# Splitting the out-projection of the SSD's even steps into two halves, one on either side of the projection of z

## The chip, the core and the metric

The kernel runs on one core of a Trainium2 chip. Its five engines work at the same time and meet through semaphores: PE (TensorE, the matrix multiplier), DVE (VectorE), ACT (ScalarE), POOL (GpSimd) and SP, which issues the DMAs. The metric is the time of one execution on the device in microseconds (us), lower being better.

## What is computed

An encoder of two layers over two request groups of 256 and 512 tokens, 768 in all, with D = 1024. The first layer mixes with a bidirectional Mamba-2 (SSD) branch, the second with neighbourhood attention. The change is in the SSD branch, which is, cut to what matters:

```python
z, xbc, dt_f, dt_b, q_mem = split(h @ w_in)
xs, bm, cm = split(silu(conv5(xbc)))                  # centred depthwise convolution, 5 taps
y = ssd_forward(xs, bm, cm, dt_f) + ssd_backward(...) + d_skip * xs
y = rmsnorm(y * silu(z), norm_g)                      # 2048 channels
x = x + rmsnorm(concat([y, m]) @ w_out)               # m: memory attention
```

Within a chunk of 128 tokens a direction is `(C B^T * decay) @ x`, and between chunks a state is carried.

## The kernel before, in words

The 2048 channels of the branch are 32 heads, taken as 16 pairs of 128 channels. The loop `for n in range(PAIRS)` of `ssd_phase` handles one pair in each step n = 0 to 15. Every matrix is multiplied in three float32r products (high*high, low*high, high*low), so a tile named `Mh`, `Wh` or `Hh` has a partner `Ml`, `Wl` or `Hl`.

Weights come in units of 512 KB. SP loads a unit into one of two slots of `Wraw` (L161 to L168), POOL splits it into `Wh` and `Wl` with two instructions (L188, L191), PE uses it and raises `unit_done`, and that lets POOL split the unit after the next. A unit is either "dense" (`pe_dense`, L200: 24 matmuls over 256 columns and 24 over 512) or half of an out-projection (`pe_out_tiles`, L251: six token tiles of six 512-column matmuls each, 36 in all). Each out tile goes to one of two PSUM banks in turn, so the third tile waits until DVE has added the first to `acc` (`out_added`, L261; the adds are L298, or copies at L296 for the first pair of channels).

An even step n from 2 on also carries the out-projection of the pairs n-2 and n-1. Before the change the order on PE in such a step is:

1. the dense unit of the next pair's x (L214), with six transposes of this pair's x (L1684) between its two parts;
2. the states (16 matmuls, L1713) and the column sums of squares (12 matmuls with one output column each, L1690);
3. the dense unit of z (L214), which ACT evicts with a SiLU;
4. `pe_out` (L280): a wait for `mix_ready`, then two halves of 36 matmuls (L264), columns 0 to 511 and 512 to 1023 of the output;
5. y (L1743 and L1747), which waits for `dec_ready`, `cs_ready` and `carried` of DVE.

On DVE the same step is: scaling x (L1536), in steps 4, 8 and 12 the masks of the group (L1552), the two operations on `seg` (L1558, L1561), `low_part(n-1)` (L1524), which makes the low part of the mixed values of pair n-1 and raises `mix_ready`, the four multiplies of `cs` (L1572), the two decay multiplies (L1577, L1578), the states carried (L1585), the adds of both halves (L298) with the four convolution taps of the next pair's x (L1168) among them, and last y (L1627), y times z (L1630) and `low_part(n)`. "The decays" below are L1577 and L1578. In the order of SP the step has the units x, z, first half, second half and then the load of the next `ab` (L1056).

Steps 2, 4, 6, 8, 10 and 12 have this form; step 14 and step 15 handle their halves in another way, which the change leaves alone.

Of the kernel before, what the change touches and what calls it, by code (L numbers as in the profile page):

```python
# [80 lines left out]
def encoder_kernel(nc, x_prompt, x_sample, mem_prompt, mem_sample, pre_g, post_g, mem_g, w_mem_kv, w_out,  # L81
# [3 lines left out]
    with ctx:  # L85
# [1201 lines left out]
        def ssd_phase(phase, pre, nxt, mixes):  # L1287
# [42 lines left out]
            def out_in(n):  # L1330
                return n % 2 == 0 and n >= 2

            def dense_index(n):
                return 4 + sum((m < LAST) + group_unit(m) + 1 for m in range(n))

# [21 lines left out]
                return evicted(dense_index(n) + (n < LAST) + group_unit(n))  # L1357

            def out_unit(n):
                return unit0 + unit_index(n) + (n < LAST) + group_unit(n) + 1  # L1360

            def sync(sp):
                load_x, load_b, load_c = pre.loads(sp)

                def load_ab(n):
                    sp.wait_ge(ab_exp, n)
                    sp.wait_ge(seg_ready, n)
                    pre.load_ab(sp, n)

                for n in range(PAIRS):  # L1370
                    if 0 < n < LAST:
                        load_x(n + 1)
                    if group_unit(n):
                        load_b(n // 4 + 1)
                        load_c(n // 4 + 1)
                    if n:
                        load_f(sp, w_in, slice(n * P, (n + 1) * P))
                    if out_in(n) and n < LAST - 1:
                        load_out(sp, 0, slice((n - 2) * P, n * P))
                    elif n >= LAST - 1:  # L1380
                        load_unit(sp, w_out[0, 12 * P:14 * P, (n % 2) * 512:(n % 2 + 1) * 512]
                                  .rearrange("(k p) c -> p k c", p=P), 2)
                    if n < LAST:
                        load_ab(n + 1)
                    if n == 1:
                        sp.wait_ge(padded, 32)
                        for rr in range(15):
                            src = bass.AP(rp_dram.tensor, (14 - rr) * 80 + 31, [[1200, HEADS], [-1, 16], [1, 32]])
                            sp.dma_start(gs_dram[:, :, rr, :], src).then_inc(expanded, 16)
                    if n == 2:  # L1390
                        for rr in range(7):
                            src = bass.AP(rp_dram.tensor, (10 - rr) * 80 + 31, [[1200, HEADS], [-1, 32], [1, 48]])
                            sp.dma_start(gp_dram[:, :, rr, :], src).then_inc(expanded, 16)
                sp.wait_ge(silu_done, x_silu(LAST))
                for i in range(3):
                    nxt.load_mem(sp, i)
                sp.wait_ge(gated, LAST)
                sp.wait_ge(x_scaled, PAIRS)
                nxt.load_mem(sp, 3)
                sp.wait_ge(ab_exp, PAIRS)  # L1400
                sp.wait_ge(seg_ready, PAIRS)
                nxt.load_mem_gain(sp)
                load_out(sp, 0, slice(14 * P, 16 * P))
# [6 lines left out]
            def scalar(act):  # L1410
# [13 lines left out]
                for n in range(PAIRS):  # L1424
                    g, a = n // 4, n % 2
                    act.wait_ge(ab_landed, 16 * (n + 1))
                    if n:
                        act.wait_ge(y_done, n)
                    else:
                        act.wait_ge(padded, 16)  # L1430
                        act.wait_ge(pre.mixed, 12)
                    for d, dst in enumerate((F_DST, B_DST)):
                        for s0, s1 in ((0, 1), (1, 4)):
                            i = act.activation(cs[:, d, :, s0:s1, :].rearrange("p h s l -> p h (s l)"),
                                               ab[:, d, :, dst[s0] * P:(dst[s1 - 1] + 1) * P], ACT.Exp)
                    i.then_inc(ab_exp, 1)

                    def decay():
                        act.wait_ge(seg_ready, n + 1)
                        for ch in range(NT):  # L1440
                            for h in range(2):
                                at = 32 + 2 * n + h
                                i = act.activation(seg[:, ch, h, :], seg[:, ch, h, :], ACT.Exp,  # L1443
                                                   bias=acs_tok[:, ch, at:at + 1])
                        i.then_inc(seg_exp, 1)

                    j = conv_index(n)
                    if n < LAST:
                        take_raw(j, n + 1)
                    decay()  # L1450
                    if n == LAST:
                        act.wait_ge(sq_summed, n)
                        take_spans(act, z, ACT.Silu)
                        U["act"].next()

                    act.wait_ge(states_done, n + 1)
                    act.activation(prev[:, 0, 0:2, :], A[2][:, 0:256].rearrange("p (s f) -> p s f", f=P), ACT.Copy)
                    act.activation(prev[:, 1, 0, :], A[3][:, 0:P], ACT.Copy)
                    act.activation(prev[:, 1, 3, :], A[3][:, 3 * P:4 * P], ACT.Copy).then_inc(prev_set, 1)
                    if next_group(n):  # L1460
                        take_bt(g + 1)

                    if group_unit(n):
                        take_raw(j + 1, g + 17)
                        silu(j, n + 1, xs[1 - a])
                        take_raw(j + 2, g + 21)
                        act.wait_ge(bc_done, g + 1)
                        silu(j + 1, g + 17, bT)
                    if n < LAST:
                        if n:  # L1470
                            act.wait_ge(sq_summed, n)
                        take_spans(act, z, ACT.Silu)
                    if group_unit(n):
                        silu(j + 2, g + 21, cT[1 - g % 2])
                    elif n < LAST:
                        silu(j, n + 1, xs[1 - a])

                    def square():
                        act.activation(z, y, ACT.Square).then_inc(sq_done, 1)

                    if n == LAST:
                        act.wait_ge(ab_exp, PAIRS)
                        nxt.mem_sums(act)
                    act.wait_ge(gated, n + 1)
                    if n < LAST:
                        square()
                    if out_in(n):
                        U["act"].next()
                        if n < LAST - 1:
                            act.wait_ge(unit_done, out_unit(n) + 2 + 2)  # L1490
                            U["act"].next()
                    act.activation(mix(n)[0], y, ACT.Copy, scale=cw[:, n + 144:n + 145]).then_inc(hi_ready, 1)
                    if n == LAST:
                        square()
# [9 lines left out]
            def vector(dve):  # L1504
# [25 lines left out]
                for n in range(PAIRS):  # L1530
# [42 lines left out]
                                                  .broadcast_to([P, 2, t1 - t0]), ALU.mult)  # L1573
                    i.then_inc(cs_ready, 1)

                    dve.wait_ge(seg_exp, n + 1)
                    c.add(dve.tensor_tensor(dec, seg, both_heads(cb_u), ALU.mult))  # L1577
                    dve.tensor_tensor(seg, seg, both_heads(cb_l), ALU.mult).then_inc(dec_ready, 1)  # L1578
# [15 lines left out]
                                else:  # L1594
                                    c.add(i)

                    j, dense = conv_index(n), dense_index(n)
                    if n == LAST:
                        nxt.mem_roots(dve, c)
                        nxt.mem_norm.dve_normed(dve, 0)  # L1600
# [2 lines left out]
                    elif n == LAST - 1:  # L1603
                        U["dve"].k = out_unit(n)
                        dve.wait_ge(dense_free, evicted(dense))
                        for i, tiles in enumerate(((0, 1), (2, 3), (4, 5), ())):
                            tap(j, n + 1, i)
                            dve_out_tiles(dve, 0, tiles)
                    elif out_in(n):
                        U["dve"].k = out_unit(n)  # L1610
                        dve.wait_ge(dense_free, evicted(dense))
                        if n == 2:
                            dve.wait_ge(stored, 16)
                        for half in range(2):
                            dve_out(dve, (half,), first=(n == 2), then=lambda k: tap(j, n + 1, 2 * half + k) if n < LAST else None)
                    elif n < LAST:
                        conv5(j, n + 1, dense)
                    if group_unit(n):
# [37 lines left out]
            def tensor(pe):  # L1656
# [39 lines left out]
                for n in range(PAIRS):  # L1696
# [21 lines left out]
                        squares(n - 1)  # L1718
                    if next_group(n):
                        turn_b(g + 1)  # L1720
                    if n < LAST:
                        for _ in range(group_unit(n) + 1):
                            pe_dense(pe)
# [5 lines left out]
                        pe_mixed(pe)  # L1729
                        pe_out_tiles(pe, range(NT))  # L1730
                    elif out_in(n):
                        pe_out(pe)

                    if n:
                        pe.wait_ge(gated, n)
# [522 lines left out]
```

## Time and profile before

| | us |
|---|---|
| median of 3 runs (lowest, highest) | 2225.23 (2225.05, 2226.71) |
| the profiled execution | 2223.82 |
| its span, first to last instruction | 2221.9 |

The span is what the profile shows; 1.9 us lie around it. A row of a timeline is: start in us from the span's start, duration in us, engine, line, operation, output and inputs, count, and in brackets the idle time before it with what ended it. A matmul's duration is longer than its distance to the next one, since matmuls are pipelined: the work is read from starts.

### The profile page before, as it was taken

To read this page: it belongs to the slowest core of one execution; us is meant where nothing else is said; L and a number is where in the kernel's file an instruction comes from. 1 tells how busy PE (TensorE), PEld (TensorE's weight loads), DVE (VectorE), ACT (ScalarE), POOL (GpSimd) and SP (SyncE) were. 2 spreads that over 40 slices of the span, in tenths; PEclk is the share of its full clock that TensorE was granted. 3 is DMA by queue.
4 is the path that set the end of the run, shared out by engine and by line. 5 is a ranking of instruction groups with operands and counts; after the bars stand their busy time and mean duration, and the time that the engine had idled before them with its cause. 6 is when DMAs were issued, how large, how long until landed. Compare 5 with 4: busy or idle time off the path is not lost.

```text
span 2221.9 us, 32088 instructions
## 1 busy us (share of the span) xinstructions
PE 2145.5 (97%) x13298; PEld 1845.3 (83%) x13298; DVE 1078.0 (49%) x1677; ACT 731.5 (33%) x1665; POOL 929.7 (42%) x623
## 2 busy tenths in 40 slices
PE   6999999999999999997999999999999999999997
PEld 5888887888888888886788887888888888888885
DVE  3103333688887888886721323234233334334236
ACT  4123122344353444343332212242324233232343
POOL 4543333332433433333753332754444445454444
PEclk9999999999999999998999999999999999999999
DMA  5221112334222232233431111322221222212211
GB/s 183 92 69 51 53 54 80 123 95 120 86 92 79 78 104 76 95 104 116 161 133 57 48 57 47 106 96 61 63 60 56 66 61 61 72 50 65 66 48 67
DMA packets 216396, 180.57 MB, mean 81 GB/s; under 512 B 23387, under 2 KB 188539, under 8 KB 216251
## 3 DMA queue, kind: packets, MB, share of 16 engines
q1 hardware_dynamic: 216251, 178.52, 25.6%
q8 instruction: 105, 1.72, 0.3%
q14 instruction: 40, 0.33, 0.1%
HBM read 168.71 MB, written 12.21 MB: 81 GB/s over the span
## 4 chain that ended last, share of the span: by engine, by line
PE 78%; DVE 15%; ACT 3%; issue 2%; DMA 1%; POOL 0%; SPq 0%; DVEq 0%; POOLq 0%; ACTq 0%
PE bank L214 44%; PE bank L264 16%; PE bank L910 4%; DVE R L1168 3%; PE bank L2143 2%; PE bank L2158 2%; PE bank L936 2%; DVE R L1536 2%; PE bank L2133 2%; PE bank L1743 1%; ACT R L1443 1%; PE bank L974 1%; DVE R L1558 1%; PE bank L1747 1%; DVE R L1578 1%
## 5 line engine op out<-in xcount | busy, mean ns | idle before, releaser
L214 PE MATMUL bank<-Hh,Wh 128*128 128x256 f32 (+1 forms) x2192 | 753.3, 344 | 7.6 <-ACT R L1107 5.1
L188 POOL TENSOR_SCALAR Wh<-Wraw 128x1024 fp32r<-128x1024 f32 x217 | 250.2, 1153 | 1215.6 <-issue 812.7
L214 PE MATMUL bank<-Hl,Wh 128*128 128x256 f32 (+1 forms) x2192 | 739.2, 337 | 0.0
L214 PE MATMUL bank<-Hh,Wl 128*128 128x256 f32 (+1 forms) x2192 | 738.0, 337 | 0.0
L191 POOL TENSOR_TENSOR Wl<-Wraw,Wh 128x1024 fp32r<-128x1024 f32 x217 | 551.0, 2539 | 18.1
L214 PEld LDWEIGHTS bank<-Hh,Wh 128*128 128x128 f32 x2192 | 417.0, 190 | 58.5 <-issue 13.6
L214 PEld LDWEIGHTS bank<-Hh,Wl 128*128 128x128 f32 x2192 | 416.5, 190 | 44.3
L214 PEld LDWEIGHTS bank<-Hl,Wh 128*128 128x128 f32 x2192 | 417.0, 190 | 41.2 <-issue 1.9
L298 DVE TENSOR_TENSOR acc<-bank,acc 128x512 f32<-128x512 f32 x240 | 164.8, 691 | 173.8 <-PE bank L264 173.1
L264 PE MATMUL bank<-Wh,Mh 128*128 128x512 f32 x528 | 210.8, 399 | 22.5 <-DVE acc L298 22.5
L264 PE MATMUL bank<-Wh,Ml 128*128 128x512 f32 x528 | 207.6, 393 | 0.0
L264 PE MATMUL bank<-Wl,Mh 128*128 128x512 f32 x528 | 207.1, 392 | 0.0
L246 ACT ACTIVATE R<-bank 128x512 f32<-128x512 f32 x78 | 46.6, 597 | 316.4 <-PE bank L214 316.4
L1168 DVE SCALAR_TENSOR_TENSOR R<-R 128x770 f32<-128x770 f32 x96 | 140.3, 1467 | 13.5 <-ACT R L1107 11.8
L264 PEld LDWEIGHTS bank<-Wh,Mh 128*128 128x128 f32 x528 | 100.0, 189 | 50.9 <-DVE acc L298 28.9
L2032 DVE TENSOR_TENSOR R<-bank,R 128x256 f32<-128x256 f32 (+1 forms) x32 | 24.9, 859 | 225.2 <-PE bank L2158 225.2
L1932 ACT ACTIVATE R<-R 128x256 f32<-128x256 f32 (+2 forms) x192 | 86.4, 452 | 137.4 <-DVE R L2058 137.4
L1902 POOL TENSOR_TENSOR R<-R 128x160 f32<-128x160 f32 (+2 forms) x160 | 108.8, 716 | 42.5 <-DVE R L2058 42.4
L2023 DVE TENSOR_SCALAR R<-R 128x256 f32<-128x256 f32 (+2 forms) x192 | 122.3, 703 | 1.1
L850 DVE TENSOR_REDUCE R<-bank 128x2 f32<-128x512 f32 x24 | 16.6, 692 | 214.6 <-PE bank L936 214.6
L264 PEld LDWEIGHTS bank<-Wl,Mh 128*128 128x128 f32 x528 | 100.3, 190 | 21.5
L264 PEld LDWEIGHTS bank<-Wh,Ml 128*128 128x128 f32 x528 | 100.3, 190 | 19.8
(232 smaller groups left out, 2726.6 us busy)
## 6 DMA issues: line engine op xcount, KB each, us to landing
Wraw<-in_na_w_in_dram SPq DMA_DIRECT2D x80, 512.0 KB, 3.6
Wraw<-in_ssd_w_in_dram SPq DMA_DIRECT2D x57, 512.0 KB, 3.8
Wraw<-in_w_out_dram SPq DMA_DIRECT2D x48, 512.0 KB, 3.5
R<-acs_dram SPq DMA_DIRECT2D x16, 1536.0 KB, 6.2
Wraw<-in_w_mem_kv_dram SPq DMA_DIRECT2D x32, 512.0 KB, 3.9
R<-gs_dram SPq DMA_DIRECT2D x32, 128.0 KB, 3.4
macc_dram<-acc SPq DMA_DIRECT2D x1, 3072.0 KB, 9.5
R<-macc_dram SPq DMA_DIRECT2D x6, 512.0 KB, 4.4
```

The lines of the kernel that those rows point to most:

```text
L188: pool.tensor_scalar(Wh[:, s, :], Wraw[:, s, :], 1.0, 1.0, ALU.mult, ALU.mult).then_inc(pool_c, 1)
L191: pool.tensor_tensor(Wl[:, s, :], Wraw[:, s, :], Wh[:, s, :].bitcast(F32), ALU.subtract)\
L214: mm = pe.matmul(DB[h.k % 2][:, 0:t1 - t0], w[:, k, :], x[:, k, t0:t1], start=(k == 0 and i == 0), stop=(k == KC - 1 and i == 2))
L246: lambda b: act.activation(dst[:, NP_:T], b[:, 0:NS], func, scale=scale)])
L264: mm = pe.matmul(A[4 + o.k % 2][:, :], x[k][:, i * P:(i + 1) * P], w[:, k, :], start=(k == 0 and j == 0), stop=(k == 1 and j == 2))
L298: dve.tensor_tensor(dst, A[4 + o.k % 2][:, :], dst, ALU.add).then_inc(out_added, 1)
L910: mm = pe.matmul(V_BANK[t][:, :], x[:, 2 * j + k, tok], y[:, k, :], start=(j == 0 and k == 0 and p == 0), stop=(j == 3 and k == 1 and p == 2))
L936: mm = pe.matmul(A[t // 2][:, (t % 2) * 256:(t % 2 + 1) * 256], qm[:, k, t * P:(t + 1) * P], kT[:, h * 2 + k, group[t] * 256:(group[t] + 1 ...
L1168: i = dve.scalar_tensor_tensor(o, x[:, k:k + w], self.cw[:, m + 24 * k:m + 24 * k + 1], o, ALU.mult, ALU.add)
L1902: i = pool.tensor_tensor(o, m, src, ALU.add)
L1932: i = act.activation(s, s, ACT.Exp, bias=nmax[:, o, h:h + 1], accum_out=sums[:, o, h:h + 1])
L2023: i = dve.tensor_scalar(s, s, rinv[:, o, h:h + 1], None, ALU.mult)
```

## The change

In the steps 2 to 12 that are even (`out_around_z`), the first half of the out-projection, with the wait for `mix_ready`, is put ahead of the dense unit of z on PE, and the second half stays behind it. SP loads the units in the order x, first half, z, second half. On DVE the first half's six adds, with two of the four taps, stand behind the multiplies of `cs` and ahead of the decays; the second half's adds with the other two taps stay where both were. ACT counts its units to match. No operation is added or left out.

```diff
+            def out_around_z(n):
+                return out_in(n) and n < LAST - 1
...
             def out_unit(n):
-                return unit0 + unit_index(n) + (n < LAST) + group_unit(n) + 1
+                return unit0 + unit_index(n) + (n < LAST) + group_unit(n) + (not out_around_z(n))
...
+                    if out_around_z(n):
+                        load_unit(sp, w_out[0, (n - 2) * P:n * P, 0:512].rearrange("(k p) c -> p k c", p=P), 2)
                     if n:
                         load_f(sp, w_in, slice(n * P, (n + 1) * P))
-                    if out_in(n) and n < LAST - 1:
-                        load_out(sp, 0, slice((n - 2) * P, n * P))
+                    if out_around_z(n):
+                        load_unit(sp, w_out[0, (n - 2) * P:n * P, 512:1024].rearrange("(k p) c -> p k c", p=P), 2)
...
                     i.then_inc(cs_ready, 1)
+
+                    j, dense = conv_index(n), dense_index(n)
+
+                    def adds(half):
+                        U["dve"].k = out_unit(n) + 2 * half
+                        dve_out(dve, (half,), first=(n == 2), then=lambda k: tap(j, n + 1, 2 * half + k))
+
+                    if out_around_z(n):
+                        dve.wait_ge(dense_free, evicted(dense))
+                        if n == 2:
+                            dve.wait_ge(stored, 16)
+                        adds(0)
 
                     dve.wait_ge(seg_exp, n + 1)
...
                     elif out_in(n):
-                        U["dve"].k = out_unit(n)
-                        dve.wait_ge(dense_free, evicted(dense))
-                        if n == 2:
-                            dve.wait_ge(stored, 16)
-                        for half in range(2):
-                            dve_out(dve, (half,), first=(n == 2), then=lambda k: tap(j, n + 1, 2 * half + k) if n < LAST else None)
+                        adds(1)
...
+                    if out_around_z(n):
+                        pe_mixed(pe)
+                        pe_out_tiles(pe, range(NT))
                     if n < LAST:
                         for _ in range(group_unit(n) + 1):
                             pe_dense(pe)
...
                     elif out_in(n):
-                        pe_out(pe)
+                        pe_out_tiles(pe, range(NT))
```

On PE, at the point in step 6 where the sums of squares end, the kernel before goes on with z (`Wh` and `Hh`, the projected input):

```order
L1713 MATMUL bank<-R 128x128 x8
L1690 MATMUL bank<-ones,R 128x1 x6
L214 MATMUL bank<-Hh,Wh 128x256
L214 MATMUL bank<-Hl,Wh 128x256
L214 MATMUL bank<-Hh,Wl 128x256
```

The changed kernel goes on with the first half (`Wh` and `Mh`, the mixed values):

```order
L1725 MATMUL bank<-R 128x128 x8
L1702 MATMUL bank<-ones,R 128x1 x6
L264 MATMUL bank<-Wh,Mh 128x512
L264 MATMUL bank<-Wh,Ml 128x512
L264 MATMUL bank<-Wl,Mh 128x512
```

Thirty-six matmuls of the out-projection now stand between the sums of squares and z; 36 are left behind z. The line numbers past the first edit have moved (L1713 is L1725, L1690 is L1702).

On DVE, step 6 from `low_part(5)` on, in the kernel before:

```order
L1524 SCALAR_TENSOR_TENSOR Ml<-R,Mh 128x768
L1572 TENSOR_TENSOR R<-R 128x2x128
L1572 TENSOR_TENSOR R<-R 128x2x384
L1572 TENSOR_TENSOR R<-R 128x2x128
L1572 TENSOR_TENSOR R<-R 128x2x384
L1577 TENSOR_TENSOR R<-R 128x1536
L1578 TENSOR_TENSOR R<-R 128x1536
L1585 SCALAR_TENSOR_TENSOR R<-R,bank 128x64 x8
L298 TENSOR_TENSOR acc<-bank,acc 128x512 x2
L1168 SCALAR_TENSOR_TENSOR R<-R 128x770
L298 TENSOR_TENSOR acc<-bank,acc 128x512 x3
```

And in the changed kernel, from the last multiply of `cs` on:

```order
L1578 TENSOR_TENSOR R<-R 128x2x384
L298 TENSOR_TENSOR acc<-bank,acc 128x512 x2
L1168 SCALAR_TENSOR_TENSOR R<-R 128x770
L298 TENSOR_TENSOR acc<-bank,acc 128x512 x3
L1168 SCALAR_TENSOR_TENSOR R<-R 128x770
L298 TENSOR_TENSOR acc<-bank,acc 128x512
L1595 TENSOR_TENSOR R<-R 128x1536
L1596 TENSOR_TENSOR R<-R 128x1536
L1603 SCALAR_TENSOR_TENSOR R<-R,bank 128x64 x8
L298 TENSOR_TENSOR acc<-bank,acc 128x512 x2
L1168 SCALAR_TENSOR_TENSOR R<-R 128x770
```

Six adds and two taps have moved ahead of the decays and of the carried states; `low_part` and the multiplies of `cs` are still ahead of every add. (L1578 of the changed kernel is L1572 of the one before.)

## Rows read from the trace of the kernel before

**Rows 1.** The page: busy time of each engine, and the chain's shares by engine.
```profile
PE 2145.5 (97%) x13298; PEld 1845.3 (83%) x13298; DVE 1078.0 (49%) x1677; ACT 731.5 (33%) x1665; POOL 929.7 (42%) x623
...
PE 78%; DVE 15%; ACT 3%; issue 2%; DMA 1%; POOL 0%; SPq 0%; DVEq 0%; POOLq 0%; ACTq 0%
```
**Rows 2.** Windows, first z matmul to first y matmul: steps 2, 4, 6, 8, 12.
```profile
core 0: us, PE busy (x) PEld busy (x) DVE busy (x) ACT busy (x) POOL busy (x), PEclk, DMA share, GB/s
504.49:529.68 25.19, 25.19 (x122) 20.59 (x121) 21.09 (x30) 5.06 (x14) 9.43 (x5) 1.00 0.62 156
573.48:603.17 29.69, 26.89 (x122) 21.72 (x122) 23.98 (x31) 6.37 (x18) 10.81 (x5) 0.94 0.33 107
663.39:688.58 25.19, 25.19 (x122) 20.59 (x121) 21.09 (x30) 5.06 (x14) 9.43 (x5) 1.00 0.30 101
732.38:759.16 26.78, 25.38 (x122) 20.58 (x121) 23.35 (x31) 6.48 (x18) 12.14 (x5) 1.00 0.37 118
...
889.75:916.23 26.48, 25.38 (x123) 20.58 (x122) 23.04 (x31) 6.48 (x18) 11.58 (x5) 1.00 0.31 100
```
**Rows 3.** Timeline of PE in step 4.
```profile
572.22 1.40 PE L1690 MATMUL bank<-ones,R 128*128 128x1 f32 x12
...
581.90 0.39 PE L264 MATMUL bank<-Wh,Mh 128*128 128x512 f32 x1
...
587.59 0.74 PE L264 MATMUL bank<-Wh,Mh 128*128 128x512 f32 x1 [2.80 <-DVE acc L298]
```
**Rows 4.** Timeline of DVE in step 4.
```profile
577.23 1.00 DVE L1524 SCALAR_TENSOR_TENSOR Ml<-R,Mh 128x768 fp32r<-128x768 f32 x1
578.16 2.49 DVE L1572 TENSOR_TENSOR R<-R 128x256 f32<-128x256 f32 x4
...
586.85 1.28 DVE L298 TENSOR_TENSOR acc<-bank,acc 128x512 f32<-128x512 f32 x2
```
**Rows 5.** Timeline of PE in step 6: the first out matmul.
```profile
671.82 0.39 PE L264 MATMUL bank<-Wh,Mh 128*128 128x512 f32 x1
```
**Rows 6.** Timeline of DVE in step 6.
```profile
661.86 1.79 DVE L1524 SCALAR_TENSOR_TENSOR Ml<-R,Mh 128x768 fp32r<-128x768 f32 x1
663.57 4.70 DVE L1572 TENSOR_TENSOR R<-R 128x256 f32<-128x256 f32 x4
668.19 1.75 DVE L1577 TENSOR_TENSOR R<-R 128x1536 f32<-128x1536 f32 x1
...
688.87 0.69 DVE L298 TENSOR_TENSOR acc<-bank,acc 128x512 f32<-128x512 f32 x1
```
**Rows 7.** Timeline of POOL in step 6.
```profile
660.70 2.14 POOL L188 TENSOR_SCALAR Wh<-Wraw 128x1024 fp32r<-128x1024 f32 x1 [10.23 <-issue]
662.93 2.99 POOL L191 TENSOR_TENSOR Wl<-Wraw,Wh 128x1024 fp32r<-128x1024 f32 x1
```
**Rows 8.** Timeline of DVE in steps 8 and 12.
```profile
736.96 2.48 DVE L1572 TENSOR_TENSOR R<-R 128x256 f32<-128x256 f32 x4
739.36 1.75 DVE L1577 TENSOR_TENSOR R<-R 128x1536 f32<-128x1536 f32 x1
...
894.02 2.48 DVE L1572 TENSOR_TENSOR R<-R 128x256 f32<-128x256 f32 x4
896.43 1.75 DVE L1577 TENSOR_TENSOR R<-R 128x1536 f32<-128x1536 f32 x1
```
**Rows 9.** Timeline of PE: two more waits, in steps 1 and 8.
```profile
477.81 0.36 PE L214 MATMUL bank<-Hh,Wh 128*128 128x256 f32 x1 [2.25 <-ACT R L1107]
...
745.09 0.50 PE L264 MATMUL bank<-Wh,Mh 128*128 128x512 f32 x1 [1.40 <-DVE acc L298]
```
**Rows 10.** Windows behind the waits of rows 3 and 9.
```profile
478.50:481.80 3.30, 3.30 (x18) 3.30 (x17) 3.23 (x4) 1.36 (x3) 2.50 (x2) 0.50 0.44 111
587.70:591.00 3.30, 3.30 (x8) 2.62 (x9) 1.80 (x3) 0.00 (x0) 0.00 (x0) 0.50 0.57 159
745.00:770.00 25.00, 24.91 (x182) 21.23 (x183) 16.00 (x21) 5.00 (x7) 8.01 (x5) 1.00 0.23 64
```

More of the change, by code:

```diff
@@ L1468, in scalar @@
                         silu(j + 1, g + 17, bT)
+                    if out_around_z(n):
+                        U["act"].next()
                     if n < LAST:
@@ L1489, in scalar @@
                         if n < LAST - 1:
-                            act.wait_ge(unit_done, out_unit(n) + 2 + 2)
-                            U["act"].next()
+                            act.wait_ge(unit_done, out_unit(n) + 3 + 2)
                     act.activation(mix(n)[0], y, ACT.Copy, scale=cw[:, n + 144:n + 145]).then_inc(hi_ready, 1)
@@ L1595, in vector @@
                                     c.add(i)
-                    j, dense = conv_index(n), dense_index(n)
                     if n == LAST:
@@ L1720, in tensor @@
                         turn_b(g + 1)
+                    if out_around_z(n):
+                        pe_mixed(pe)
+                        pe_out_tiles(pe, range(NT))
                     if n < LAST:
```

## The prediction

> **What bounds the kernel now.** I read the page first: PE is busy for 97% of the span and holds 78% of the chain that ended last [rows 1]. So the kernel ends when PE ends, and an edit that only moves instructions can do no more than open or close waits of PE. Next I took the windows of the changed steps, from the first matmul of z to the first of y, which hold the same work in each: z and 72 matmuls of the out-projection. They take 25.19 us in steps 2 and 6 (step 10 is alike), but 29.69, 26.78 and 26.48 in steps 4, 8 and 12 [rows 2]. Taking 25.19 as the time without waits, before loses 4.50 + 1.59 + 1.29 = 7.4 us there. That is all that the change can win in these windows.
>
> The timelines say what the loss is. In step 4 the first out tile begins at 581.90, and the third after a wait of 2.80 us for DVE's first add [rows 3]; that add is late because `low_part`, the multiplies of `cs`, the decays and the carried states stand ahead of it, and the adds begin at 586.85 [rows 4]. Steps 8 and 12 show the same with 1.40 (the row of step 8 is in [rows 9]). In steps 2, 6 and 10 DVE is in time.
>
> **What the change does, part by part.** *Work.* Nothing is added: the same matmuls, adds, taps and loads. Their durations count for nothing but through waits. *Loads and splits.* A unit keeps its place in the row of units and only the content of the second and third changes, so POOL's splits start at the same events (the end of the unit two before). I cost this at 0: the second unit of a step is split before the step's first ends, whatever it holds. *ACT* takes z some 8.4 us later (from the start of z at 663.39 [rows 2] to the first out matmul at 671.82 [rows 5] is 8.43 for a dense unit, and (25.19 - 8.43)/2 = 8.38 for a half), and DVE needs z only behind y, which comes another half later: 0. *The decays* must be done before y. Behind the last add of the first half they have z and the second half on PE, 16.8 us, as cover. With the carried states they lie in step 4 between 580.65 and 586.85 [rows 4], 6.2 us with a split of POOL beside them: 0 for y. They also stand ahead of the second half's adds; that is weighed below.
>
> *The first half's start.* It needs `mix_ready`, which `low_part` of the pair before raises; the edit moves the wait ahead of z and moves nothing on DVE ahead of `low_part`. This is where the change costs. In step 4 the squares begin at 572.22 and z at 573.48; `low_part` ends at 577.23 + 1.00 = 578.23 [rows 3, 4]. z now covers none of that time: PE stands for 4.7 us, with z, the second half and y queued behind it in order. In steps 8 and 12 `low_part` ends where the multiplies of `cs` begin, at 737.0 and 894.1 [rows 8], against 732.38 and 889.75 for z before [rows 2]: waits of 4.7 and 4.4 us. In step 6 it ends at 663.65 against 663.39 [rows 2, 6]: 0.3 us; steps 2 and 10 are alike to 0.05 us (the same pattern, read from the same view).
>
> *The third tile.* It needs the first add, which now stands right behind the multiplies of `cs`. An add takes 0.69 us [rows 6], and PE followed the add in step 4 by 0.05 us (586.85 + 0.69 = 587.54, next matmul 587.59) [rows 3, 4]. A tile is 8.38/6 = 1.40 us, so without a wait the third starts 2.79 us behind the first. The delay of a whole first half is then the start of its third tile less (start of z before + 2.79):
> - Step 6: the adds can start where L1577 did, 668.19 [rows 6]; third tile at 668.19 + 0.69 + 0.05 = 668.93, less 666.18 = 2.75. Steps 2 and 10 the same: 8.25 for three.
> - Step 4: the multiplies are done at 580.65 and the next operation could start at 580.57 (rows overlap by 0.08) [rows 4]; third tile at 581.31 less 576.27 = 5.04.
> - Step 8: 739.36 + 0.74 = 740.10, less 735.17 = 4.93 [rows 8]. Step 12: 896.43 + 0.74 = 897.17, less 892.54 = 4.63 [rows 8].
>
> The sum is 22.85 us. Later tiles do not wait again: an add and a tap make 1.7 us for two tiles of 1.4. The old waits disappear, since z stands between the halves and the decays lie beside it: -7.4. Net +15.4 us before the clock is counted.
>
> *The clock.* Behind the waits of 2.25 us in step 1 and of 2.80 in step 4 PE's granted clock is 0.50, the lower of its two levels (1.2 GHz), for at least 3.3 us; behind the 1.40 in step 8 it stays at 1.00 [rows 9, 10]. In step 4 that cost 4.50 less the wait itself (587.59 - 581.90 - 2.79 = 2.90), so 1.60 us [rows 2, 3]. The new waits: one of 4.4 to 4.7 us in each of steps 4, 8 and 12, and one of about 2.3 us (0.2 more ahead of it) in each of 2, 6 and 10 (the second tile's end near 666.6, the third's start at 668.93). The cost of the clock behind each lies between 0 and, if it stays low twice as long, 3.2. All six are at or above the 2.25 that was followed by a slow stretch, so I take 1.60 each, 9.6 in all. Part of a slow stretch can fall within the longer waits, where it costs nothing; for that I take off 1.5 in all, my choice, about one stretch of the six.
>
> **The sum.** 2223.82 (the profiled execution) + 15.4 + 9.6 = 2248.8; the median of the runs shown is 1.4 above that execution, 2250.2; less the 1.5 just named, 2248.7. I forecast 2249 us, +1.1%.
>
> **A rule weighed.** POOL's split began as x's unit ended in step 6, and both engines ran long: L191 took 2.99 us, and the four multiplies took 4.70 us against 2.49 in step 4 [rows 4, 6, 7]. L191 ran until 665.92, so the multiplies that began at 663.57 had 2.2 us to lose, and 2.2 is what they lost. The Trainium skill, "SBUF — State Buffer", section "SBUF: two separate sides", says that VectorE instructions with two SBUF inputs and GpSimd share one pair of ports under an exclusive lock, held for a whole instruction, while the loser waits. By that rule, with which the trace agrees, the change can do harm in a second place, since the decays now start just as the first half's end releases a split; what that would make is rival 4.
>
> **Rivals.**
> 1. *The waits come, the clock does not fall behind the short ones.* For it: 2.3 us is right at the shortest that was followed by a slow stretch, 2.25 [rows 9, 10]. Then 3 x 1.60 go: 2223.8 + 15.4 + 4.8 + 1.4 = 2245.4. With none anywhere: 2240.6.
> 2. *POOL no longer meets the multiplies in steps 2, 6, 10.* Then these take 2.49 instead of 4.70, and the third tile is late by 0.5 instead of 2.75: -6.7, and what is left of the short waits is too short for the clock, -4.8; from 2250.2 that makes 2238.7. Against it: the split and the multiplies both hang on the end of x's unit, which does not move.
> 3. *Faster: the first half's start is not late.* Place: the wait for `mix_ready` in steps 4, 8, 12. If DVE reached `low_part` there by the end of the squares, and the multiplies of `cs` did not hold the first add, PE would lose nothing where it now loses 7.4: 2217.8. It decides from the point where the six first halves lose less than 7.4 us together, 1.2 each; by the rows they lose 2.75 to 5.04. Against it: DVE does not start a changed step earlier than before, since the last add follows PE's last tile in both orders (688.87 + 0.69 against 688.58 for y in step 6 [rows 2, 6]).
> 4. *Worse: the decays hold the second half, and the clock stays low for longer.* The decays and carried states begin 1.0 us behind the first half's end (the last add ends at 689.56 where the halves end at 688.58 [rows 2, 6]) and take 6.2 us as in step 4: done at 7.2. The second half's third tile is due 8.43 + 2.79 = 11.2 us behind that end and its add must begin 0.74 sooner, at 10.5, so 3.3 us are spare. A whole further L188 and L191 (2.14 + 2.99 [rows 7]) would use them up and make 1.8 us late in each step, 11 in six; one of the two would not. Beside it each long wait could bring twice the slow stretch: +4.8. So 2253.5 with the clock alone, up to 2264 with both. Against the first: step 4's 6.2 us have a split in them already.
> 5. *The change is not what it says.* The rows of the order show the 36 matmuls and the six adds moved, so I give this nothing of its own.
>
> **Chances and range.** Forecast with its clock (2246 to 2252) 0.55; rival 1 0.22; rival 2 0.07; rival 4 0.09; rival 3 0.03; 0.04 for something that levels out to no change. A measurement of this kernel can tell about 0.2%, 4.5 us, from no change. Slower than that are the forecast and rivals 1, 2 and 4: 0.93. The range from 2238 to 2256 takes in rivals 1 and 2 and the nearer part of 4, and leaves out rival 3, no change, and the far part of 4.
>
> **What would show it.** In the profile after: PE idle 4 to 5 us ahead of the first L264 in steps 4, 8 and 12, ended by DVE's `low_part`; about 2.3 us ahead of the third tile in steps 2, 6 and 10, ended by the add; no wait of PE in any second half; about 23 us of such delay against 7.4; and granted clock 0.50 behind these waits, five stretches more than before. I am wrong if PE's first L264 follows the squares at once in step 4, if the decays or y come to hold PE, or if the time is under 2235.

## The result, and the profile after

| | us |
|---|---|
| before, median of 4 runs (lowest, highest) | 2225.97 (2225.05, 2227.89) |
| after, median of 4 runs (lowest, highest) | 2248.95 (2248.44, 2251.52) |
| ratio, with its 95% interval | 1.0104 [1.0087, 1.0122] |
| span of the profiled execution, before and after | 2221.9 and 2247.0 |

The change costs 1.0%. The page after, where [rows 1] were, has the same instructions:

```profile
PE 2153.9 (96%) x13298; PEld 1851.2 (82%) x13298; DVE 1092.4 (49%) x1677; ACT 731.7 (33%) x1665; POOL 932.5 (42%) x623
```

PE gives up a point of its share. The windows of the changed steps say where. They begin where z would begin without a wait, which is 1.26 us behind the start of the sums of squares (as in [rows 3], 572.22, and [rows 2], 573.48), and end at the first matmul of y, so they hold the same work as [rows 2]. Columns as there:

```profile
506.12:533.98 27.86, 25.50 (x123) 20.72 (x122) 23.12 (x30) 5.05 (x14) 10.78 (x5) 1.00 0.58 139
577.77:609.38 31.61, 27.00 (x123) 22.07 (x122) 25.54 (x31) 6.48 (x18) 10.42 (x5) 0.89 0.32 101
669.62:699.04 29.42, 27.06 (x122) 21.88 (x121) 23.11 (x30) 5.05 (x14) 10.78 (x5) 0.94 0.26 87
744.38:776.03 31.65, 27.46 (x123) 22.39 (x122) 25.11 (x31) 6.47 (x18) 11.73 (x5) 0.89 0.31 100
836.27:865.74 29.47, 27.11 (x122) 21.85 (x121) 23.10 (x30) 5.05 (x14) 10.77 (x5) 0.94 0.25 86
910.69:942.81 32.12, 27.93 (x123) 22.76 (x122) 25.11 (x31) 6.47 (x18) 11.73 (x5) 0.89 0.25 82
```

Less 25.19 each, the six steps lose 2.67, 6.42, 4.23, 6.46, 4.28 and 6.93 us, 31.0 in all, against 7.4 before. That is 23.6 of the 25.1 us between the spans. The rest lies outside the windows: PE was 1.6 us later already at the sums of squares of step 1 (459.00 against 457.38), which the change does not reach. That is the spread of single executions: in e1 below, the same up to there, the squares begin at 457.51.

PE's waits in steps 2 to 12 carry these names (totals of PE's waits between 425 and 980 us; the second and third count the adds and, in step 2, the copies):

```profile
PE bank L264 <- DVE Ml L1530: 13.5, 6, 4.6
...
PE bank L264 <- DVE acc L298: 4.4, 2, 2.2
...
PE bank L264 <- DVE acc L296: 2.2, 1, 2.2
```

L1530 is `low_part` (L1524 before). PE's timeline of steps 4 and 6 has them one by one; they answer to [rows 3] and [rows 5]:

```profile
576.51 1.40 PE L1702 MATMUL bank<-ones,R 128*128 128x1 f32 x12
582.52 0.79 PE L264 MATMUL bank<-Wh,Mh 128*128 128x512 f32 x1 [4.61 <-DVE Ml L1530]
```
```profile
668.36 1.40 PE L1702 MATMUL bank<-ones,R 128*128 128x1 f32 x12
669.93 0.50 PE L264 MATMUL bank<-Wh,Mh 128*128 128x512 f32 x1 [0.17 <-DVE Ml L1530]
...
675.14 0.79 PE L264 MATMUL bank<-Wh,Mh 128*128 128x512 f32 x1 [2.19 <-DVE acc L298]
```

The second half has no wait in any step. DVE in step 6, as in [rows 6], shows who ends the wait and what follows; POOL's rows beside it answer to [rows 7]:

```profile
668.08 1.79 DVE L1530 SCALAR_TENSOR_TENSOR Ml<-R,Mh 128x768 fp32r<-128x768 f32 x1
669.80 4.69 DVE L1578 TENSOR_TENSOR R<-R 128x256 f32<-128x256 f32 x4
674.41 1.28 DVE L298 TENSOR_TENSOR acc<-bank,acc 128x512 f32<-128x512 f32 x2
...
683.39 1.90 DVE L1595 TENSOR_TENSOR R<-R 128x1536 f32<-128x1536 f32 x1
685.21 3.95 DVE L1596 TENSOR_TENSOR R<-R 128x1536 f32<-128x1536 f32 x1
689.09 1.73 DVE L1603 SCALAR_TENSOR_TENSOR R<-R,bank 128x64 f32<-128x64 f32 x8
```
```profile
669.15 2.98 POOL L191 TENSOR_TENSOR Wl<-Wraw,Wh 128x1024 fp32r<-128x1024 f32 x1
682.63 1.05 POOL L188 TENSOR_SCALAR Wh<-Wraw 128x1024 fp32r<-128x1024 f32 x1 [10.50 <-issue]
683.77 3.77 POOL L191 TENSOR_TENSOR Wl<-Wraw,Wh 128x1024 fp32r<-128x1024 f32 x1
...
692.10 2.40 POOL L191 TENSOR_TENSOR Wl<-Wraw,Wh 128x1024 fp32r<-128x1024 f32 x1
```

The first add waits for four multiplies that L191 stretches to 4.69 us, just as in [rows 6]. The granted clock (third column from the right, as in [rows 10]) in the five stretches where it is low:

```profile
579.40:586.20 6.80, 3.67 (x9) 2.90 (x10) 6.12 (x7) 4.21 (x15) 0.53 (x1) 0.51 0.48 172
675.00:678.30 3.30, 3.16 (x8) 2.48 (x9) 1.74 (x4) 0.00 (x0) 0.00 (x0) 0.51 0.24 72
746.70:753.40 6.70, 4.69 (x11) 3.73 (x12) 5.06 (x6) 3.17 (x12) 1.14 (x1) 0.51 0.89 313
842.30:845.60 3.30, 3.30 (x9) 2.58 (x9) 1.65 (x3) 0.00 (x0) 0.00 (x0) 0.51 0.05 16
913.90:920.70 6.80, 5.68 (x13) 4.46 (x14) 4.32 (x7) 2.28 (x9) 0.25 (x1) 0.51 0.76 270
```

Step 2 has none, although its wait is as long as that of step 6 (2.19 us both).

### The profile page after: what moved, and what is told of

Its sections match the earlier page's. It is cut to its first block, busy times and chain, and to the rows that moved or that the text cites. A ratio compares the mean times of both kernels' runs of the same rounds, so it can differ in the third digit from the quotient of the medians.

```text
span 2247.0 us, 32088 instructions
## 1 busy us (share of the span) xinstructions
PE 2153.9 (96%) x13298; PEld 1851.2 (82%) x13298; DVE 1092.4 (49%) x1677; ACT 731.7 (33%) x1665; POOL 932.5 (42%) x623
## 4 chain that ended last, share of the span: by engine, by line
PE 77%; DVE 16%; ACT 3%; issue 3%; DMA 1%; POOL 0%; SPq 0%; DVEq 0%; POOLq 0%; ACTq 0%
PE bank L214 43%; PE bank L264 16%; PE bank L910 4%; DVE R L1168 3%; DVE R L1542 2%; PE bank L2158 2%; PE bank L2173 2%; PE bank L936 2%; PE bank L2148 2%; PE bank L1758 1%; DVE R L1564 1%; PE bank L974 1%; DVE R L1578 1%; ACT R L1448 1%; DVE Ml L1530 1%
## 5 line engine op out<-in xcount | busy, mean ns | idle before, releaser
L188 POOL TENSOR_SCALAR Wh<-Wraw 128x1024 fp32r<-128x1024 f32 x217 | 244.4, 1126 | 1237.7 <-issue 849.5
L191 POOL TENSOR_TENSOR Wl<-Wraw,Wh 128x1024 fp32r<-128x1024 f32 x217 | 559.7, 2579 | 18.1
```

The costliest lines, as they stand in the source:

```text
L188: pool.tensor_scalar(Wh[:, s, :], Wraw[:, s, :], 1.0, 1.0, ALU.mult, ALU.mult).then_inc(pool_c, 1)
L191: pool.tensor_tensor(Wl[:, s, :], Wraw[:, s, :], Wh[:, s, :].bitcast(F32), ALU.subtract)\
```

## The experiments

Every kernel below ran beside the kernel before on the same chip; its ratio is to that. The delay per step is worked out from each trace as above: from the start of the sums of squares to the first matmul of y, less 26.45 us (662.13 to 688.58, step 6 of the kernel before). The 26.45 us are not quite free of small gaps, so values can lie a little below zero: in step 6 of e8 the 72 out matmuls take 16.54 us (8.29 + 8.25) where they took 16.76 before, and z 8.35 where it took 8.43.

| kernel | steps 2, 4, 6, 8, 10, 12: delay, us | sum | ratio to before [95%] |
|---|---|---|---|
| before | 0.0, 4.5, 0.0, 1.6, 0.1, 1.3 | 7.4 | 1 |
| changed | 2.7, 6.4, 4.2, 6.5, 4.3, 6.9 | 31.0 | 1.0104 [1.0087, 1.0122] |
| e1 adds early | 0.8, 6.5, 0.7, 7.7, 0.8, 7.4 | 23.9 | 1.0083 [1.0067, 1.0099] |
| e2 low part early | 4.0, 6.6, 4.2, 5.7, 4.1, 6.8 | 31.3 | 1.0103 [1.0085, 1.0122] |
| e3 both early | 0.8, 2.2, 0.4, 2.2, 0.4, 2.2 | 8.2 | 1.0006 [0.9996, 1.0016] |
| e4 PE filled | 2.7, 4.6, 2.8, 4.6, 2.7, 4.6 | 22.1 | 1.0087 [1.0072, 1.0102] |
| e5 PE's move alone | 9.3, 12.0, 10.2, 12.6, 10.3, 11.9 | 66.3 | 1.0256 [1.0240, 1.0273] |
| e6 DVE's move alone | 7.8, 8.6, 7.7, 8.6, 7.7, 7.8 | 48.2 | 1.0194 [1.0172, 1.0215] |
| e7 woven | 2.2, 2.2, 2.1, 2.2, 2.2, 2.2 | 13.1 | 1.0038 [1.0024, 1.0052] |
| e8 carried states split | -0.3, 0.3, -0.3, 0.3, -0.3, 0.3 | 0.0 | 0.9966 [0.9953, 0.9978] |
| e9 split only | -0.3, 1.5, -0.3, 1.5, -0.3, 1.5 | 3.5 | 0.9980 [0.9970, 0.9990] |

**e1: the first adds ahead of the multiplies of cs.**

```diff
+                    if out_around_z(n):
+                        ...
+                        adds(0)
                     dve.wait_ge(ab_exp, n + 1)
...
-                    if out_around_z(n):
-                        ...
-                        adds(0)
                     dve.wait_ge(seg_exp, n + 1)
```

> The changed kernel, with the first half's adds also ahead of the multiplies of cs (before: behind them). Theory A (in steps 2, 6, 10 PE waits at the third tile because the first add stands behind these multiplies; in 4, 8, 12 the wait for mix_ready dominates): the 2.2 us waits go, the waits of 4.2 to 4.6 us ahead of the first half stay. 3 x 2.5 + 3 x 0.2 us and two slow stretches of 1.6 less: about 2238, up to 2245 if the decays, now later still, hold the second half. Theory B (all of the loss hangs on mix_ready): 2249, no change.

Median 2241.52. Steps 2, 6 and 10 fall from 2.7, 4.2, 4.3 to 0.7 or 0.8; steps 4, 8, 12 keep theirs or lose a little more (7.7 against 6.5 in step 8), with the wait for `low_part` (4.20 us in step 4). Theory A holds, B does not. A wait of 0.38 us has come into every second half: the multiplies of cs now lie with the decays, and the second half's first add is late.

**e2: low_part early.**

```diff
+                    if n and n % 2 == 0:
+                        low_part(n - 1)
                     if n % 4 == 0:
                         dve.wait_ge(bc_done, g + 1)
...
-                    if n and n % 2 == 0:
-                        low_part(n - 1)
```

> The changed kernel, with low_part(n-1) moved from behind the two operations on seg to right behind the scaling of x, so mix_ready comes 4 to 9 us earlier. Theory A (third tile is bound by the first add behind cs, whose place in time hardly moves): the idle time of 4.2 to 4.6 us ahead of the first half in steps 4, 8, 12 goes and comes back as one of about the same length at the third tile; 2247 to 2250. Theory B (mix_ready is the cost): three waits of 4.3 us and three slow stretches go, 13 to 18 us: 2231 to 2236.

Median 2247.12, delay 31.3 against 31.0 us. The wait for `mix_ready` has gone and its time stands one event later. PE and DVE in step 4:

```profile
584.76 0.80 PE L264 MATMUL bank<-Wh,Mh 128*128 128x512 f32 x1 [3.92 <-DVE acc L298]
```
```profile
577.86 3.83 DVE L1570 TENSOR_TENSOR R<-R 128x1536 f32<-128x1536 f32 x1
581.62 2.48 DVE L1579 TENSOR_TENSOR R<-R 128x256 f32<-128x256 f32 x4
584.02 1.28 DVE L298 TENSOR_TENSOR acc<-bank,acc 128x512 f32<-128x512 f32 x2
```

The 4.61 us ended by `low_part` in the changed kernel are 3.92 ended by the first add here. So removing the longest wait that the profile names need not pay by itself. The equal sums hide one shift: the wait at the third tile of steps 2, 6 and 10 is now 2.49 us, and in step 2 the clock falls behind it too (delay 4.0 against 2.7), while step 8 loses 0.8 less.

**e3: both.** The two edits above in one kernel.

> Both moves together: low_part(n-1) right behind the scaling of x, then the operations on seg, then the first half's adds, then the multiplies of cs and the decays. Theory A: nothing waits in steps 2, 6, 10; in 4, 8, 12 the third tile still waits about 2.5 us for seg's operations, which stand ahead of the adds: 7.6 us of delay and up to three slow stretches: 2226 to 2236, most likely 2230, so no gain over the kernel before. Theory C (the two moves hide each other's cost, and DVE's order is all): under 2222.

Median 2223.48, the same as before within 0.2%, and between what the two theories expected: A's waits are there but shorter (1.55 us at the third tile and not 2.5), and the granted clock is 1.00 in all six windows. e1 took 7.1 us of delay, e2 none, both together 22.8, the clock's part included: each late event hid behind the other in steps 4, 8 and 12. What is left in step 4 is a wait of 1.55 us at the third tile, with the operations on `seg` still ahead of the adds, and 0.38 us in the second half:

```profile
580.13 0.50 PE L264 MATMUL bank<-Wh,Mh 128*128 128x512 f32 x1 [1.55 <-DVE acc L298]
...
597.31 0.50 PE L264 MATMUL bank<-Wh,Mh 128*128 128x512 f32 x1 [0.38 <-DVE acc L298]
```

**e4: PE kept at work.** The kernel computes 81 extra products, 18 in each of three steps and 9 in each of the other three.

```diff
+                def filler(count):
+                    h = HF["pe"]
+                    pe.wait_ge(dense_free, h.value + 1)
+                    for _ in range(count):
+                        pe.matmul(DB[h.k % 2][:, :], Hh[:, 0, 0:P], Hh[:, 0, 0:512], start=True, stop=True)
...
                     if out_around_z(n):
+                        if n % 4 == 0:
+                            filler(18)
                         pe_mixed(pe)
-                        pe_out_tiles(pe, range(NT))
+                        pe_out_tiles(pe, (0, 1))
+                        if n % 4 == 2:
+                            filler(9)
+                        pe_out_tiles(pe, (2, 3, 4, 5))
```

> The changed kernel with PE kept at work during its waits: 18 extra matmuls of 512 columns into a free PSUM bank ahead of the wait for mix_ready in steps 4, 8, 12, and 9 of them between the second and third tile of the first half in steps 2, 6, 10. They leave every wait where it ends now and their output is overwritten. If the clock costs what I said (8.4 us over five slow stretches), these stretches go and the time falls by 7 to 9 us: about 2241. If the clock costs nothing: 2249. If the fillers reach past a wait's end by a matmul or two: up to 2 us more.

Median 2242.62. The windows of steps 4 and 6 (begun and ended as for the changed kernel):

```profile
578.86:608.68 29.82, 29.70 (x140) 23.94 (x140) 25.09 (x31) 6.48 (x18) 11.79 (x5) 1.00 0.34 106
668.92:696.86 27.94, 27.50 (x131) 22.41 (x131) 23.11 (x30) 5.06 (x14) 10.78 (x5) 1.00 0.27 91
```

The granted clock is 1.00 in all six windows and their delay is 22.1 us, 8.9 less, while `low_part` and the first add come where they did, counted from the squares, within 0.4 us. So about 22 of the 31 us are waits and 9 the lower clock. In the times this is less sure: the medians are 6.3 us apart, but the two kernels were timed in different groups, and their intervals to the kernel before overlap.

**e5 and e6: one half of the change each.** e5 puts the call of the first adds behind the carried states in the changed kernel; e6 leaves PE, SP and ACT as before and moves the adds only:

```diff
 e5
-                        adds(0)
                     dve.wait_ge(seg_exp, n + 1)
...
+                        adds(0)
                     if n == LAST:
 e6 (from the kernel before)
                     i.then_inc(cs_ready, 1)
+                    if out_two:
+                        ...
+                        adds(0)
                     dve.wait_ge(seg_exp, n + 1)
...
-                        for half in range(2):
-                            dve_out(dve, (half,), ...)
+                        adds(1)
```

> The changed kernel with the first half's adds put back behind the decays and the carried states; PE, SP and ACT as changed. So it is the change without its part on DVE. By the rows of the kernel before the first add then comes 5.1 us later in steps 2, 6, 10 and 4.7 to 6.3 later in 4, 8, 12: 54 us of delay in the six steps where the changed kernel has 23, with more slow stretches: 2273 to 2285. If the place of the first adds on DVE did not matter: 2249.

> The kernel before on PE, SP and ACT (z first, then both halves), with only the first half's adds moved ahead of the decays on DVE. Theory A: the waits of steps 4, 8, 12 in the first half go, but now the decays and the carried states lie between the halves with no z to cover them, and the second half's third tile waits 4 to 5 us in each of the six steps: 24 to 31 us and up to six slow stretches against 7.4 before: 2246 to 2258. Rival (the move on DVE is the good half of the change and the one on PE the bad one): 2218.

Medians 2280.14 and 2266.46. e5 came as expected; in its step 6 the third tile waits 7.20 us. e6 was expected at 2246 to 2258 and is beyond that: the rival is plainly wrong, and theory A's size was too small. Its waits in the second half are 6.2 us and not 4 to 5. DVE and POOL in step 6, between the halves:

```profile
697.41 1.90 DVE L1590 TENSOR_TENSOR R<-R 128x1536 f32<-128x1536 f32 x1
699.24 3.89 DVE L1591 TENSOR_TENSOR R<-R 128x1536 f32<-128x1536 f32 x1
703.05 1.74 DVE L1598 SCALAR_TENSOR_TENSOR R<-R,bank 128x64 f32<-128x64 f32 x8
704.70 1.28 DVE L298 TENSOR_TENSOR acc<-bank,acc 128x512 f32<-128x512 f32 x2
```
```profile
697.79 3.72 POOL L191 TENSOR_TENSOR Wl<-Wraw,Wh 128x1024 fp32r<-128x1024 f32 x1
```

The second decay takes 3.89 us and not 1.75, since the first half's end starts the split that stands in its way, every time. Neither half of the change is the good one: each alone is worse than both.

**e7: adds woven with the operations on seg.**

```diff
+                        adds(0, (0, 1))
                     c.link(... seg, first operation)
+                        adds(0, (2, 3))
                     ... seg, second operation
+                        adds(0, (4, 5))
                     ... cs
+                        tap(j, n + 1, 0)
...
-                        adds(1)
+                        adds(1, range(NT), lambda k: tap(j, n + 1, 1 + k))
+                        tap(j, n + 1, 3)
```

> PE, SP and ACT as in the changed kernel; on DVE low_part(n-1) right behind the scaling of x, then adds 0 and 1, the first operation on seg, adds 2 and 3, the second operation on seg, adds 4 and 5, the multiplies of cs, the first tap, the decays, the carried states, and the second half's adds with taps two and three among them and tap four behind. By theory A each add now comes in time for its tile in all six steps; 0 to 1 us is lost per step where the decays run late: 2218 to 2224, better than the kernel before by up to 7 us. If the time is above 2230, something else than the order of DVE holds the first half.

Median 2230.83: the expectation missed, and it had said that above 2230 something else than DVE's order holds the first half. The rows do not show that: every wait in the six windows still ends with an add of DVE. The long waits are gone, but every one of the six steps has two small ones, 0.45 us in the first half, where an add stands behind a 1.75 us operation on `seg`, and 1.45 in the second:

```profile
672.41 0.50 PE L264 MATMUL bank<-Wh,Mh 128*128 128x512 f32 x1 [0.45 <-DVE acc L298]
...
687.94 0.50 PE L264 MATMUL bank<-Wh,Mh 128*128 128x512 f32 x1 [1.45 <-DVE acc L298]
```

Against e3, steps 4, 8 and 12 gain nothing (1.55 + 0.38 became 0.45 + 1.45), and steps 2, 6 and 10, which e3 had almost cured, lose 1.4 to 1.8 us more each. What is put among the first adds pushes cs, the decays and the carried states towards the second half's first add, whose time is as fixed.

**e8 and e9: the second half's turn.** Order of e3, with `carried` cut in two groups of four:

```diff
                     for at, (fwd, bwd) in enumerate(...):
+                        if around:
+                            U["dve"].k = out_unit(n) + 2
+                            adds(1, ((0, 1), (2, 3))[at])
...
-                        adds(1)
+                        adds(1, (4,))
+                        tap(j, n + 1, 2)
+                        adds(1, (5,))
+                        tap(j, n + 1, 3)
```

and in e8 alone, between the two operations on `seg`:

```diff
+                        if n % 4 == 0:
+                            adds(0, (0, 1))
```

> The order of e3, with two more moves on DVE. The carried states are cut in two groups of four, which stand behind adds 0 and 1 and behind adds 2 and 3 of the second half instead of ahead of both, with the last two taps behind adds 4 and 5; and in steps 4, 8, 12 adds 0 and 1 of the first half stand between the two operations on seg. e3's profile has a wait of 0.38 us in every second half, which ends with an add behind the carried states, and one of 1.5 us at the third tile of steps 4, 8, 12, ended by an add behind seg. By theory A both go: 8.2 us of delay in e3 become 0 to 2: 2218 to 2220 where the kernel before has 2224, ratio about 0.997. If the same as before or slower, PE is held by something that DVE's order does not reach.

> As e8 with only the first of its two moves, so seg's operations both stand ahead of the first half's adds in all steps. Theory A: the 0.38 us of six second halves go (2.3 us), the 1.5 us at the third tile of steps 4, 8, 12 stay, with the third more that these steps lost in e3: 5 to 6 us of delay in all, 1 to 2 us under the kernel before: ratio 0.999.

e9's median is 2219.89, e8's 2217.55, both clear of 1 and in the order expected, though their intervals overlap, so that the times alone do not show which is better; e9's delay, 3.5 us, is less than the 5 to 6 expected. e8's window of step 6:

```profile
662.33:687.22 24.89, 24.89 (x123) 20.74 (x122) 19.76 (x29) 6.48 (x18) 9.87 (x5) 1.00 0.32 106
```

PE is busy through the whole of it. In steps 4, 8 and 12 one wait of 0.33 us is left. This order beats the kernel before by 0.34%, 7.4 us between the medians (2224.98 and 2217.55), which is all that the six windows had to give.

## Why the prediction was right

The forecast was 2249 us, and 2248.95 was measured. Step by step:

- *The wait for `mix_ready`*: forecast 4.7, 4.7 and 4.4 us in steps 4, 8, 12 and 0.3 in the others; measured 4.75, 4.33, 4.33 and 0.31 from where z would begin to the first half's start. (The brackets say 4.61, 4.19, 4.19 and 0.17, since they count from the end of the matmul before.) By e2 it is real but not decisive: had it been the only cost, e2 would have been 13 to 18 us faster.
- *The third tile*: forecast 2.75 us of delay in steps 2, 6, 10, of which 2.3 wait; measured 2.7 (step 2, and all three in e4) and 2.19. e1 and e2 together show that the sum had to be taken, as it was, at the third tile, where the later of two events decides.
- *The sum of waits*: forecast 22.85 us; 22.1 in e4, where the clock is out of it. The prediction gave 1.40 us as the old wait in step 12 too; it is 1.10, and the sum, which went by the windows, does not rest on it.
- *The clock*: forecast 9.6 less 1.5, 8.1 us, from six stretches; found 9 (31.0 less 22.1), from five. Step 2's wait of 2.19 us brought none, the same wait in steps 6 and 10 did; and each long wait brought a stretch of 6.8 us, part of it inside the wait (582.52 - 579.40 = 3.1 us in step 4). Step by step, the changed kernel less e4, the clock costs 1.5 and 1.6 us in steps 6 and 10, the 1.60 taken from the old stretch, but 1.8, 1.9 and 2.3 in steps 4, 8 and 12, where I had taken 1.5 off in all. The count and the lengths were off in opposite ways. That the sum met is in part luck.
- *No cost in the second half*: right, there is no wait. The reason had less room than I gave it. I took the decays and the carried states at 6.2 us; they take from 683.39 to 690.82, 7.4, since L191 of the split always meets the second decay (3.95 against 1.75 us). Done 8.5 us behind the first half's end, they still come ahead of the 10.5 at which the add was due, so rival 4 found no stall to make. The Trainium skill, "SBUF — State Buffer", section "SBUF: two separate sides", was right to weigh: by its lock one engine waits out the other's instruction. The trace agrees, 3.95 and 3.77 us where 1.75 and 2.40 stand without a collision: L191 ends at 687.54, 2.25 behind the first decay (685.29), and the second decay at 689.16, 1.6 behind L191.
- *Rival 3* (a gain of the 7.4 us) was wrong for this order of DVE. e8 shows that its ceiling was right: with `low_part`, adds and carried states moved as well, the gain is 7.4 us.

What stays open is what decides between a slow stretch and none behind a wait of 2.2 us.

## What to carry to other kernels

When a consumer is moved ahead of work that covered its inputs, list every event it waits for, with the time each happens now, and sum at the last one; removing the event that the profile names can leave the time as it is, as e2 did. Producer and consumer orders are one edit: each half of this change alone cost 1.9% and 2.6%, both 1.0%, and the order made for it gained 0.3%. Here an in-order engine that had to serve two fixed deadlines was fitted by cutting one item and setting the deadline's work between the pieces (the carried states in e8 and e9); moving whole items from one side of a deadline to the other (e1, e7) moved the wait with them.

## What the hardware showed that I had not expected

Waits of PE of the same 2.19 us were followed by the lower clock (0.51 granted, its 1.2 GHz level) in steps 6 and 10 and not in step 2. Waits of 4.2 to 4.6 us brought 6.8 us of it, 3.7 to 5.7 us of that with PE at work, where one of 2.80 had brought 3.3 [rows 3, 10]. And a collision of DVE and POOL that hangs on the same event recurs in all six steps: 3.95 or 3.89 us for an operation of 1.75, in the changed kernel and in e6. Another order only moves it: in step 4 of e3 both decays take 1.75 us, and the multiplies of cs, now the ones beside the split, 4.85 and not 2.49.
